# The first groups of a state-space mixer in another order: tanh of x, z of group 2, splits and taps

## What is computed

```
zxbcdt = x @ w_in                      # z, xbc, dt
xbc = silu(depthwise_conv(xbc, conv_w) + conv_b)      # 5 taps; x, B, C
y_diag = einsum(cb, decay, xdt)        # cb = C B^T of a chunk of 128 tokens, decay = exp of sums
y_off  = einsum(cc, prev, exp(a_cs))   # the other chunk's state
y = y_fwd + y_bwd + d_skip * xs
y = y * silu(z)
out = grouped_rmsnorm(y, norm_w) @ w_out
```

## Time and profile before

| | us |
|---|---|
| runs (three) | 1474.38, 1475.82, 1477.06; median 1475.82 |
| profiled execution | 1469.49, its span 1467.8 |
| TensorE matmul busy | 1405.8 (96%) |
| VectorE busy | 1041.8 (71%) |
| ScalarE busy | 759.4 (52%) |
| GpSimd busy | 198.4 (14%) |
| first mixer, second mixer | about 0 to 250, about 1038 to 1270 |

### The profile page before, as it was taken

One profiled execution on the slowest core, in us unless ns is written; L12 is line 12 of the kernel. 1 busy time (PEld: TensorE's weight loads), 2 busy tenths in 40 slices (PEclk: granted clock), 3 DMA queues, 4 the chain that ended last, 5 costly groups with the idle time before them and its releaser, 6 DMA issues. The chain is left out here.

```text
span 1467.8 us, 22867 instructions
## 1 busy us (share of the span) xinstructions
PE 1405.8 (96%) x8939; PEld 1270.2 (87%) x8939; DVE 1041.8 (71%) x1337; ACT 759.4 (52%) x1121; POOL 198.4 (14%) x245
## 2 busy tenths in 40 slices
PE   7899999999999999999999999999988999999996
PEld 7898997988889989888899798888988999798885
DVE  5889899666577485556856666567788898856555
ACT  4777776344434335444355444443586877354440
POOL 2223222522220000000000000000032121200000
PEclk9899999999999999999999999999999999999998
DMA  9755663667656556555544446555764655365530
GB/s 291 245 172 174 200 194 120 192 210 200 203 178 226 174 169 206 200 190 184 200 144 144 144 173 200 185 188 162 214 206 146 201 175 170 128 212 180 199 143 29
DMA packets 198186, 266.86 MB, mean 182 GB/s; under 512 B 11768, under 2 KB 167824, under 8 KB 198080
## 3 DMA queue, kind: packets, MB, share of 16 engines
q1 hardware_dynamic: 188720, 237.72, 49.7%
q0 software_dynamic: 9200, 27.55, 6.6%
q10 hardware_dynamic: 160, 0.13, 0.0%
HBM read 264.19 MB, written 1.18 MB: 181 GB/s over the span
## 5 line engine op out<-in xcount | busy, mean ns | idle before, releaser
L1557 DVE TENSOR_TENSOR w_low<-raw,w_high 128x2048 fp32r<-128x2048 f32 (+1 forms) x226 | 512.8, 2277 | 64.4 <-ACT w_high L1153 52.6
L1153 ACT ACTIVATE w_high<-raw 128x2048 fp32r<-128x2048 f32 (+1 forms) x226 | 427.5, 1896 | 168.3 <-PE y L777 141.7
L777 PE MATMUL y<-w_high,opT 128*128 128x512 f32 x1408 | 397.3, 391 | 0.1
L603 PE MATMUL acc<-xT,w_high 128*128 128x256 f32 x1856 | 344.6, 287 | 3.4 <-DVE w_low L1557 3.4
L777 PEld LDWEIGHTS y<-w_high,opT 128*128 128x128 f32 x1408 | 259.3, 188 | 51.3 <-issue 1.2
L603 PEld LDWEIGHTS acc<-xT,w_high 128*128 128x128 f32 x1856 | 292.9, 194 | 5.3 <-issue 4.9
L603 PE MATMUL acc<-xT,w_low 128*128 128x256 f32 x928 | 264.4, 285 | 0.0
L777 PE MATMUL y<-w_low,opT 128*128 128x512 f32 x704 | 222.6, 390 | 0.0
L1576 DVE TENSOR_TENSOR opT<-conv,opT 128x512 fp32r<-128x512 f32 x56 | 40.4, 721 | 224.4 <-issue 202.4
L624 PE MATMUL acc<-w_high,xT 128*128 128x256 f32 (+1 forms) x928 | 175.2, 291 | 9.3 <-DVE xT L1621 9.3
L603 PEld LDWEIGHTS acc<-xT,w_low 128*128 128x128 f32 x928 | 179.9, 194 | 0.0
(11 more groups left out here) (217 smaller groups left out, 1621.1 us busy)
## 6 DMA issues: line engine op xcount, KB each, us to landing
raw<-in_ffn_w_in SPq DMA_DIRECT2D x128, 512.0 KB, 4.7
raw<-in_ffn_w_out SPq DMA_DIRECT2D x128, 512.0 KB, 4.3
raw<-in_ssd_w_in SPq DMA_DIRECT2D x96, 512.0 KB, 5.1
raw<-in_ssd_w_out SPq DMA_DIRECT2D x32, 512.0 KB, 4.5
E<-cumsum_dram POOLq DMA_DIRECT2D x32, 512.0 KB, 5.1
raw<-in_sc_w_in SPq DMA_DIRECT2D x24, 512.0 KB, 4.6
raw<-in_na_w_qkv SPq DMA_DIRECT2D x24, 512.0 KB, 4.6
raw<-in_sc_w_out SPq DMA_DIRECT2D x8, 512.0 KB, 4.1
```

The costliest lines, as they stand in the source:

```text
L603: mm = nc.tensor.matmul(bank[:, c * SEQ:(c + 1) * SEQ][:, span], w[:, col:col + P], xT[:, k, low, span], start=(k == 0 and part == 0), sto ...
L777: mm = nc.tensor.matmul(Y[t][c][:, :], opT[:, o % ACTS, low, k, t * P:(t + 1) * P], w[:, k * D + c * 512:k * D + (c + 1) * 512], start=(fi ...
L1153: nc.scalar.activation(w_high[:, u % SPLIT, c0:k * c], raw[:, u % RAW, c0:k * c], ACT.Copy).then_inc(w_high_done, 1)
L1557: V.tensor_tensor(w_low[:, u % RAW, c0:k * c], raw[:, u % RAW, c0:k * c], f(w_high[:, u % SPLIT, c0:k * c]), ALU.subtract).then_inc(w_low_ ...
```

## The change

On TensorE the projection of z of group 2 is issued ahead of the cross product and the scan of group 0, instead of behind them. On ScalarE the tanh of x of group 0 no longer stands between the two halves of the shift of the decay rows; the shift is done in one piece behind the copies, and the tanh of bc 1 and the start of x 1 come ahead of the exponents. The high part of unit first+8 is made earlier. In the loop's branch for group 2, x 2 is started ahead of the tanh of bc 2. On VectorE the split of first+7 and the taps of bc 1 come ahead of the join of group 0, the split of first+8 ahead of the products of group 0, both taps of group 2 ahead of their silus, the split of first+12 behind the silus; and the split of first+14 moves out of the branch for i = 2 into the next `split_to`, behind the products of group 2. No instruction is added or removed.

```diff
@@ TensorE
+                    project(names[("z", 2)], range(NT))
                     cross_chunk(0)
                     scan(0)
                     for i in range(2, G - 1):
-                        project(names[("z", i)], range(NT))
+                        if i > 2:
+                            project(names[("z", i)], range(NT))
@@ ScalarE
                     start_conv("x", 0)
-                    shift_heads(0, early)
+                    split_to(first + 8)
                     conv_tanh()
-                    shift_heads(0, late).then_inc(e_shifted, 1)
                     start_conv("bc", 1)
                     copy_cross(0)
                     copy_xs(0)
+                    shift_decays(0)
+                    conv_tanh()
+                    start_conv("x", 1)
                     decays(0, early)
                     decays(0, late)
-                    conv_tanh()
-                    start_conv("x", 1)
-                    split_to(first + 8)
                     shift_decays(1)
@@ ScalarE, i == 2
                             normalise(1)
-                            conv_tanh()
+                            start_conv("x", 2)
+                            conv_tanh(1)
                             gated_high(1)
-                            start_conv("x", 2)
                             split_to(names[("x", 2)] + 4)
                             conv_tanh()
@@ VectorE
                     silu_x(0, y)
+                    split_to(first + 7)
+                    y = taps("bc", 1)
                     join_decays(0)
-                    y = taps("bc", 1)
+                    silu_bc(1, y)
+                    split_to(first + 8)
                     decayed_products(0)
-                    split_to(first + 7)
-                    silu_bc(1, y)
                     y = taps("x", 1)
                     scale_cross(0)
                     silu_x(1, y)
-                    split_to(first + 8)
                     join_decays(1)
@@ VectorE, i == 2
-                            y = taps("bc", 2)
+                            bc = taps("bc", 2)
                             rms_known(1)
+                            y = taps("x", 2)
+                            silu_bc(2, bc)
+                            silu_x(2, y)
                             split_to(names[("bc", 2)] + 4)
-                            silu_bc(2, y)
                             gated_low(1)
-                            silu_x(2, taps("x", 2))
                             join_decays(2)
@@ VectorE, end of the loop's body
-                        if i < G - 2:
+                        if 2 < i < G - 2:
                             split_to(names[("so", i - 2)] + 4)
```

## The result

The changed kernel takes 1460.02 us (median of six executions, 1457.40 to 1462.52) against 1474.71 us (six executions, 1471.09 to 1477.06) for the kernel before on the same chip: a ratio of 0.990, with a 95% interval of 0.9883 to 0.9918. It is 14.7 us faster. The forecast was 10.0 us faster, 1465.8 us; the sign was right, the time lies at the very edge of the wide range (1460.0 to 1472.5) and outside the forecast's own (1463.5 to 1469), and a third of the gain was missing from the sum.

What follows compares the result with a forecast made beforehand. The chain over VectorE and ScalarE, not TensorE's lead, was taken to decide each mixer's end. 5.2 - 2.5 + 9.1 - 1.8 = 10.0 us off the median 1475.82 gave 1465.8 us; range 1460.0 to 1472.5, its own 1463.5 to 1469.

Steps and rivals of the forecast that it cites:

- The chain: Work over VectorE and ScalarE, said to decide each mixer's end; summed from silu of x 1 to scaling of group 2.
- rival (c): Both mixers: the chain is not the bound and TensorE keeps all it wins, 19 us, giving 1457 us; chance 0.05.
- the sign that I had set against it: Group 7: waits at the turn of x staying at 1.4 us would mean rival (c) holds.
- clock term: Half clock behind new waits: 2.5 us at group 1, first mixer; 1.8 us at group 7, second mixer; 0 elsewhere.
- Part 1: Group 0: tanh of x ahead of the decay rows; wait 1.49 becomes 0.66 us, second mixer's 3.72 us goes.
- the price is paid by the decays: First mixer, group 0: decays shifted later, so VectorE gives the products at 66.8, 3.2 us later than before.
- Part 2: z of group 2 ahead of first scan: scan waits 1.6 and 0 us; new waits 2.9 and 2.2 us for x 1.
- Part 3: VectorE of group 2 and split of unit 14: scaling of group 2 earlier; 5.2 us won first mixer, 9.1 second.
- Rival (e): Half clock does not end after the turn of x 1 in both mixers: slower, 1482.5 us; chance 0.04.
- the same rest: Second mixer: chain gains other than silu of x 1's 2.95 us, as in the first; scaling 8.2 us earlier.
- sum of 10.0 us: Both mixers: 5.2 - 2.5 + 9.1 - 1.8 us, taken off the median 1475.82 us.
- Rival (a): The clock holds through all new waits: 14.3 us won, 1461.5 us; chance 0.17.

Runs made afterwards that it cites:

- z alone: Kernel before with only the projection of z of group 2 moved ahead of the cross product of group 0 on TensorE: 1480.78 us, ratio 1.006.
- tanh alone: Kernel before with only the new order of groups 0 and 1 on ScalarE and VectorE: 1475.70 us, ratio 1.0019.
- unit 14 alone: Kernel before with only the split of unit first+14 moved out of the branch for group 2: 1467.26 us, ratio 0.9969.
- the last run: Changed kernel with turn of x 1 inside bc 2, splits first+12 and first+15 moved, and gated_low(1) ahead of split first+12: 1460.45 us, ratio 0.9916.
- second profile: Profiled execution from timing the unaltered changed kernel again: span 1458.1 us; that timing's median 1460.99 us, ratio 0.9909 to the kernel before.
- unit 14 back: Changed kernel with only the split of unit first+14 back in the branch for group 2: 1467.79 us, ratio 0.9966 to the kernel before.
- z back: Changed kernel with only the projection of z of group 2 back behind the first scan: 1468.36 us, ratio 0.9972 to the kernel before.
- the kernel before with 1.31 us left of it: Kernel before with the cross product of group 2 done three times, inside the wait ahead of group 2's scan: 1471.76 us, ratio 0.9989.
- the kernel with the turn inside: Changed kernel with the turn of x 1 between the two halves of bc 2's projection: 1456.99 us, timed again 1459.21 us.
- where it was filled: Changed kernel with 16 unread matmuls ahead of the turn of x 1 and 15 ahead of that of x 7: 1460.66 us, ratio 0.9906.

## Why the forecast was right and where it failed

**What bounds the kernel.** Right. The chain was named as the limit, against rival (c) in which TensorE keeps all it wins (1457 us). The 1460.0 us measured lies closer to (c)'s number than to mine, but its mechanism did not happen: the waits at group 7 grew from 1.46 and 1.41 to 2.27 and 2.30 us (said: 2.5 and 3.3), which is the sign that I had set against it, and the scaling of group 2 came 2.3 us earlier in the first mixer counted from the sums (126.25 - 34.90 = 91.35 before, 126.27 - 37.21 = 89.06 after), about the 2.7 that the chain gives with its clock term. Timelines of VectorE (the silu of x 1) and of ScalarE (the scaling of group 2) in the changed kernel, both mixers:

```profile
74.55 0.69 DVE L1719 SCALAR_TENSOR_TENSOR xsT<-tanh,conv 128x512 f32<-128x512 f32 x1
...
1082.27 0.69 DVE L1719 SCALAR_TENSOR_TENSOR xsT<-tanh,conv 128x512 f32<-128x512 f32 x1 [0.17 <-ACT tanh L1244]
```

```profile
126.27 0.91 ACT L1309 ACTIVATE gate<-gate,small 128x256 f32<-128x256 f32 x2
...
1132.91 0.91 ACT L1309 ACTIVATE gate<-gate,small 128x256 f32<-128x256 f32 x2
```

The firmest sign of the chain: from that scaling to the turn of x 7 every profile of this document takes 104.9 to 105.1 us, wherever TensorE waited before. The exceptions are the second mixers of before (106.3), z alone and tanh alone (106.5), where the forecast had put 0.9 us that VectorE stands for TensorE; it was 1.3.

**Part 1** held. The turn of x 0 waits 0.64 us in the first mixer (said: 0.66) and not in the second. That it pays nothing alone was in the text only as "the price is paid by the decays"; tanh alone, 1475.70 us, shows it.

**Part 2** held in its places and nearly in its sizes. First scan: 1.98 us (said 1.6) and none. Wait for the silu of x 1: 0.88 and 2.48 us (said 2.9 and 2.2). In the first mixer both together are 2.9 us where I had 4.5, because the scan and the state products ran at half clock (2.82 and 2.02 us instead of 1.89 and 1.08 in the second mixer), so that TensorE reached the turn later. The taps of x 1 took what I had charged, 4.04 us. Timelines of VectorE and GpSimd in the changed kernel, first the eight taps together, then the second of them by itself:

```profile
69.81 4.04 DVE L1707 SCALAR_TENSOR_TENSOR conv<-conv_pad,ssd_par,conv 128x256 f32<-128x256 f32 x8
...
70.21 1.26 DVE L1707 SCALAR_TENSOR_TENSOR conv<-conv_pad,ssd_par,conv 128x256 f32<-128x256 f32 x1
```

```profile
69.98 1.21 POOL L459 TENSOR_TENSOR ring_b<-ring_b,own_token 128x512 f32<-128x512 f32 x1 [9.29 <-DVE own_token L1758]
```

The whole excess of 0.79 us over the taps alone (3.25) lies in one instruction. Seven of the eight take 0.47 or 0.48 us; the one that starts at 70.21, inside the GpSimd product, takes 1.26 and ends at 71.47, 0.28 us after the product's end at 71.19. The Trainium skill ("SBUF — State Buffer", on the shared port) makes the loser wait for the whole instruction, and the trace agrees: that tap waits until the product is through. The 0.79 is less than 1.21 because the product began while the tap before still ran. The other direction agrees too: a GpSimd instruction of 0.19 us lay 1.82 us, until VectorE's split ended at 124.05. So the forecast's remark that the row fits a partial overlap, and that nothing tells the two apart, missed what the taps one by one show.

What I failed to see is that z's move rests on the moved split of its weights. The parts do not add: by the ratios z alone +8.8 us, tanh alone +2.8, unit 14 alone -4.6, and all together -13 to -15.

**Part 3** held. No wait before the scan of group 2; 0.95 and 0.87 us at the turn of its gated rows (said 1.7); the stand for unit 14 gone. One new wait was not foreseen: 0.53 and 0.52 us at the turn of x 2. Its bank is freed by `gated_low(1)`, and that now stands behind a split. It costs nothing that the chain does not cost already: with the wait taken away (the last run) the time did not change, though 1.14 us for a split came in its place.

**The sum by stretches.** In both mixers one link was too optimistic: counted from the sums, the silu of x 1 starts 0.84 us later than before in the first mixer (said 0.35) and 2.1 us earlier in the second (said 2.95). The rest of the chain to the scaling came within 0.1 us of the sum in the first mixer and in the second mixer's second profile. First mixer: 5.2 less 2.5 for the clock is 2.7; measured 2.3 at the scaling and 2.4 at the turn of x 7. Second: 9.1; measured 7.2 and, in the second profile, 8.7. The profile with 7.2 has half clock behind the turn of x 1 (1084 to 1087.4), which I had put at 0 of 0 to 3.2; the one with 8.7 has none there. Group 7, second mixer: half clock in the first profile, as said, none in the second; the first mixer's, put at 0, came in both. "Half clock over more than 7 us at a time" was a sign that I would be wrong, and a stretch of 10.2 us did come; it was no more harmful than the 3.2 us allowed for it. Rival (e) needed 29 us of half clock in these places, and they had 20.4 (10.2 and three times 3.4). Two slips of arithmetic change nothing: the second mixer's idle time and half clock add up to 14.8, not 14.5 us, and "the same rest" would give 8.5, not 8.2 us, at its scaling.

So the sum of 10.0 us is about right for equal clocks. That can be read from the timed executions themselves. Those of the kernel before at a mean clock of 0.987 have a median of 1470.5 us (14 executions), those of the changed kernel at 0.987 1461.4 us (five): 9.1 us apart.

**The step that failed** is the carrying over to the median, and with it the clock term. I wrote that the median is 6.3 us above the profiled execution, and took the same 10.0 us off both. That supposes that the two kernels' executions stray alike from their profiles. They do not: the median of before lies 5.2 us above its profiled execution (1474.71 against 1469.49), that of the changed kernel 2.5 us below its own (1460.02 against 1462.52), and with the 7.0 us between the two profiled ones this is the 14.7. Another 1.1 us of the miss is the level: before had a median of 1475.82 in the three runs that I started from, 1474.71 in six. Before, the executions at 0.984 (19, median 1474.5 us) and 0.985 (14, 1472.7) are more than half of the 56, and the profiled one at 0.987 was among the fastest; it also had the earliest start of all profiles, 34.90 us against 35.3 to 37.5. The changed kernel's eleven lie at 0.987 to 0.991, and its first profiled execution was its slowest. The clock had two signs in this change: the new waits bring half clock, which I priced at 4.3 us, and the removed waits take half clock away; for that the sum has no term of its own beyond what the chain of that one fast execution holds. In the medians the mean clock went up, from 0.985 to 0.989: 0.004 of 1460 us, about 6 us. 9.1 and 6 make 15, against 13.0 to 14.7 measured.

Which removed wait does this? The kernels that keep the 3 us wait before the scan of group 2 in both mixers have clocks of 0.985 (before), 0.982 (z alone), 0.984 (tanh alone) and 0.9845 (unit 14 back). Those without it have 0.987 (unit 14 alone), 0.9885 (z back) and 0.989 (changed), and the kernel before with 1.31 us left of it has 0.987. Unit 14 back against the changed kernel is the clean pair: one line, 0.0045 of clock and 7 to 10 us, of which the chain explains 2.9 to 4.4. Z back has waits of 7.73 and 5.36 us elsewhere and still 0.9885, so it is not the length of the idle time alone. Two things stay open. No trace exists of a slower execution of the kernel before (0.984), so where its further half clock lies was not seen. And the same short waits are followed by half clock in one execution and not in another. In the middle layers TensorE waits for VectorE in every profile, here 1.36 and 0.84 us, one 2.2 us behind the other. Changed kernel, first profile, the second of these waits and the window around it:

```profile
843.51 0.48 PE L624 MATMUL acc<-w_high,xT 128*128 128x256 f32 x2 [0.84 <-DVE xT L1622]
...
842.00:846.00 4.00, 3.15 (x26) 2.94 (x26) 2.14 (x3) 3.00 (x3) 0.00 (x0) 1.00 0.67 230
```

The same in its second profile:

```profile
842.22 0.63 PE L624 MATMUL acc<-w_high,xT 128*128 128x256 f32 x2 [0.84 <-DVE xT L1622]
...
842.00:846.00 4.00, 3.78 (x19) 3.81 (x20) 2.83 (x3) 1.81 (x2) 0.00 (x0) 0.57 0.32 106
```

What decides between the two is open. The scattered stretches near 260, 550, 842, 1036 and 1265 us all begin at such waits or within 3 us of them, and the change touches none of these.

Rival (a), the clock holding everywhere, gave 1461.5 us and was nearest in number, 1.5 us off; (c) was 3 us off. For (a) that is luck. Its number fits the median, but its reason is wrong, since the clock did fall behind the new waits, in the profile at four places.

## What to carry to other kernels

Make the sum between landmarks of one profiled execution, and don't carry it to a median as it is: look first at the mean clock of the timed executions beside the profiled one's, since a change that removes a wait of 3 us can also remove half clock that the one trace did not have. Before a projection is moved ahead of a wait, look up on every engine what it needs itself; here the same move cost 8.8 us without one weight split on VectorE moved too, and gained at least 7 us with it. When TensorE's idle places move from one instruction to the next and the stretch keeps its length, stop rearranging TensorE: the chain on the other engines is what has to become shorter.

## What the runs showed of the hardware

- **A mean clock that differs from execution to execution.** The same kernel on the same input ran at mean clocks of 0.982 to 0.988, with median times from 1474.5 us (at 0.984) to 1470.5 (at 0.987).
- **How long half clock lasts behind the same wait.** A wait of 1.98 us ahead of the first scan was followed by half clock in every version with the new order of z. It lasted 10.2 us where a second wait of 0.7 to 0.9 us fell inside it (three profiles), 6.8 us where that second wait was moved out of it (the kernel with the turn inside, both profiles), and 3.4 us where it was filled.
- **Short waits and chance.** Waits of 2.27 to 2.29 us at the turn of x 7 of the first mixer were followed by 3.4 us at half clock in both profiles of the changed kernel and by none in the first profile of the kernel with the turn inside. Of two waits of 1.31 and 1.32 us in one execution only the first was; waits of 1.36 and 0.84 us, 2.2 us apart, were in one profile of the changed kernel and not in the other.
- **The start.** The second token tile's arrival ended TensorE's wait at 8.86 us in the profile of before and at 10.41 in that of the changed kernel, with the same instructions ahead of it, and the first sums came at 34.90 and 37.21 us, 2.3 us apart; the 0.8 us that this adds to the tile's 1.55 was not traced. Over all profiles the first sums lie between 34.90 and 37.46 us.
- **A VectorE instruction that starts inside a GpSimd product** of 1.21 us took 1.26 us instead of 0.47, and ended 0.28 us after the product; the seven beside it were as short as ever.
- **A small GpSimd instruction beside a large one of VectorE.** Two elements per partition, 0.19 us alone, took 1.82 us beside a split of 2.28 us, and ScalarE's scaling waited 1.57 us behind it.
